# Two attentions of a four-layer network: the modulation product put one step later, a weight split one step sooner, and half a weight split behind the next row maxima

## The reference, cut to what matters

```python
for l in range(2):                                   # first network
    mod_lat = silu(c) @ w_ada[l] + b_ada[l]          # modulation: shift, scale, gate
    mod_ctx = silu(c_ctx) @ w_ada[l] + b_ada[l]
    xn = rms_norm(x, g_norm[l]) * (1 + sc) + sh      # the same for the context rows
    a, b, c_ = split_proj(xn @ w_in[l])              # three branches
    y_b = attend(q_rows, k_all, v_all) * silu(bz)    # softmax attention, 8 heads of 64
    x = x + gt * (concat([y_a, y_b, y_c]) @ w_out[l])
x = rms_norm(x, g_final)
# second network, layer 0: causal attention, 16 heads of 64, with rotation of q and k
qkv = (rms_norm(h) @ w_qkv).reshape(B, S, 3, 16, 64)
q, k = apply_rope(qkv[:, :, 0]), apply_rope(qkv[:, :, 1])
o = softmax(mask(q @ k.T / 8)) @ v
h = h + o @ w_o                                      # then a gated feed-forward layer
# layer 1: latent attention and a second feed-forward layer
```

## Time and profile before

| | |
|---|---|
| median of 3 runs | 1080.47 us (1080.44 to 1082.03) |
| profiled execution, whole | 1080.5 us |
| its span | 1078.6 us |
| PE / DVE / ACT / POOL busy | 99% / 67% / 53% / 13% |
| first attention, steps 0 to 18 | about 194 to 270 us |
| second attention | about 487 to 576 us |

### The profile page before, as it was taken

The page is one execution under the profiler, slowest core; times in us unless marked ns, Lnnn a source line. Parts: engine busy times, 40 slices in busy tenths (PEclk is TensorE's granted clock), DMA queues, the critical chain, the costliest instruction groups (busy, mean ns, idle before and its releaser), DMA issues.

```text
span 1078.6 us, 19909 instructions
## 1 busy us (share of the span) xinstructions
PE 1067.6 (99%) x8094; PEld 950.8 (88%) x8094; DVE 717.5 (67%) x1223; ACT 572.1 (53%) x970; POOL 141.2 (13%) x166
## 2 busy tenths in 40 slices
PE   9999999999999999999999999999999999999998
PEld 7887878656898998799899999999997799999997
DVE  4664566386554868768865676666677776766674
ACT  4532666544444566766565554444574555444454
POOL 0000010253210000632531000000023410000000
PEclk9999999999999999999999999999999999999999
DMA  9732221287513442057454364555543334555551
GB/s 384 315 126 74 77 78 40 94 286 250 189 43 118 143 141 79 2 196 234 147 167 153 121 235 160 193 184 172 195 154 112 124 118 157 196 195 174 214 180 39
DMA packets 25386, 168.77 MB, mean 156 GB/s; under 512 B 3280, under 2 KB 3536, under 8 KB 5456
## 3 DMA queue, kind: packets, MB, share of 16 engines
q1 hardware_dynamic: 25152, 167.25, 43.9%
q10 hardware_dynamic: 144, 0.26, 0.1%
HBM read 164.35 MB, written 1.05 MB: 153 GB/s over the span
## 4 chain that ended last, share of the span: by engine, by line
PE 91%; DVE 3%; ACT 2%; POOL 1%; DMA 1%; issue 1%; SPq 0%; DVEq 0%; ACTq 0%
PE bank L421 25%; PE bank L422 25%; PE bank L423 24%; PE bank L1633 2%; PE bank L478 2%; PE bank L1498 2%; PE bank L1653 2%; PE bank L1643 1%; DVE wlo L415 1%; DMA raw<-in_stream 1%; PE bank L1525 1%; PE bank L2296 1%; POOL TILE L1594 1%; ACT TILE L1687 1%; PE bank L1516 1%
## 5 line engine op out<-in xcount | busy, mean ns | idle before, releaser
L421 PE MATMUL bank<-OPH,whi 128*128 128x256 f32 (+1 forms) x1716 | 519.8, 303 | 0.6 <-DVE wlo L415 0.3
L423 PE MATMUL bank<-OPH,wlo 128*128 128x256 f32 (+1 forms) x1716 | 511.2, 298 | 0.0
L422 PE MATMUL bank<-OPL,whi 128*128 128x256 f32 (+1 forms) x1716 | 511.2, 298 | 0.0
L415 DVE TENSOR_TENSOR wlo<-raw,whi 128x1024 fp32r<-128x1024 f32 (+1 forms) x256 | 305.5, 1236 | 103.5 <-ACT whi L400 103.4
L421 PEld LDWEIGHTS bank<-OPH,whi 128*128 128x128 f32 x1716 | 328.0, 191 | 18.3 <-issue 5.6
L422 PEld LDWEIGHTS bank<-OPL,whi 128*128 128x128 f32 x1716 | 328.1, 191 | 9.9 <-issue 1.2
L423 PEld LDWEIGHTS bank<-OPH,wlo 128*128 128x128 f32 x1716 | 328.0, 191 | 9.8
L400 ACT ACTIVATE whi<-raw 128x1024 fp32r<-128x1024 f32 (+1 forms) x256 | 255.9, 1050 | 73.2 <-PE bank L423 72.4
L421 PE MATMUL bank<-whi,OPH 128*128 128x256 f32 (+2 forms) x272 | 93.7, 344 | 0.6 <-DVE OPL L695 0.6
L422 PE MATMUL bank<-wlo,OPH 128*128 128x256 f32 (+2 forms) x272 | 91.1, 335 | 0.0
L423 PE MATMUL bank<-whi,OPL 128*128 128x256 f32 (+2 forms) x272 | 91.0, 335 | 0.0
(11 more groups left out here) (279 smaller groups left out, 1122.4 us busy)
## 6 DMA issues: line engine op xcount, KB each, us to landing
raw<-in_stream SPq DMA_DIRECT2D x143, 1024.0 KB, 4.9
PROJ<-in_stream SPq DMA_DIRECT2D x5, 1024.0 KB, 18.0
raw<-in_stream SPq DMA_DIRECT2D x4, 1056.0 KB, 7.7
PROJ<-PROJ SPq DMA_DIRECT2D x32, 64.0 KB, 3.8
FIRST<-in_first SPq DMA_DIRECT2D x1, 1248.0 KB, 6.1
C<-in_con SPq DMA_DIRECT2D x1, 1157.5 KB, 7.3
FIRST<-in_first SPq DMA_DIRECT2D x1, 1024.0 KB, 8.1
WST<-in_w_s SPq DMA_DIRECT2D x2, 256.0 KB, 7.4
```

The source lines that it names most:

```text
L415: nc.vector.tensor_tensor(c.w[1][:, part], c.raw[:, part], c.w[0][:, part].bitcast(F32), ALU.subtract).then_inc(*raises(c.lo[h]))
L421: nc.tensor.matmul(out, w[0], x[0], start=start, stop=False, skip_group_check=skip)
L422: nc.tensor.matmul(out, w[0], x[1], start=False, stop=False, skip_group_check=skip)
L423: return nc.tensor.matmul(out, w[1], x[0], start=False, stop=stop, skip_group_check=skip)
```

## The change

The modulation step n now stands in attention step n+1 instead of n. The first `whi` half of `w_out` chunk 0 stands in modulation step 13 for ACT and its `wlo` half in step 14 for DVE, instead of both in step 15: in attention steps 14 and 15 instead of 15. In the second attention the DVE part of `q3` is parted: one half of `wlo` stays where it was, the other stands behind the maxima of pair 4.

```diff
             def step(self, e, who, n):
+                if who == "act" and n == self.steps - 4:
+                    split_hi(e, self.after.s + 0.5)
                 if who == "dve":
+                    if n == self.steps - 3:
+                        split_lo(e, self.after.s + 0.5)
                     if n % 2 == 0 and n > 0:
                         self.pairs[n // 2 - 1].add_bias(e)
                     if n % 2:
                         self.pairs[n // 2].copy_rows(e)
-                split = split_hi if who == "act" else split_lo
-                if n == self.steps - 2:
-                    split(e, self.after.s + 0.5)
...
-            def split_next(e, who, j):
+            def split_next(e, who, j, less=0):
                 if j.frees_head:
                     split_ahead(e, who, j.head[1].s + 1 + SPLIT)
                 for c, *_ in j.parts:
                     if c is not None and c.used == j.u.full:
-                        split_ahead(e, who, c.s + 1 + SPLIT)
+                        split_ahead(e, who, c.s + 1 + SPLIT - less)
...
+                if what == "half" and who == "dve":
+                    self.product.split_next(e, who, self.product.jobs[i], 0.5)
...
-                if l == 0 and j < mod.steps:
-                    attend_step(f"attn{l}_chunk", "chunk", mod, j)
+                if l == 0 and 0 < j <= mod.steps:
+                    attend_step(f"attn{l}_chunk", "chunk", mod, j - 1)
...
+        half_low = [(qkv_jobs, ("half", qkv.at["q3"]))]
-                F("q3"), w_(1), A("q3"), s_(3), Ra(2), Ra(6), Rb(2), Rb(6), t_(2), n_(3), M(XN[3]), V_("q3"),
-                F("k3"), A("k3"), s_(4), t_(3), V_("k3"), n_(4),
+                F("q3"), w_(1), A("q3"), s_(3), Ra(2), Ra(6), Rb(2), Rb(6), t_(2), n_(3), M(XN[3]), half_low,
+                F("k3"), A("k3"), s_(4), V_("q3"), t_(3), V_("k3"), n_(4),
```

## The result

| | before | changed |
|---|---|---|
| median | 1080.47 us (5 runs, 1080.44 to 1082.03) | 1085.45 us (5 runs, 1084.09 to 1086.93) |
| profiled execution, its span | 1080.5, 1078.6 us | 1085.69, 1083.9 us |
| mean granted clock of TensorE, single runs | 0.999 to 1.000 | 0.995, 0.997, 0.997, 0.998, 0.995 |

The changed kernel is slower by 4.98 us, ratio 1.0043, 95% interval 1.0033 to 1.0054. The sign was forecast; the size was twice the forecast (+2.45), and the time lies outside the range.

A forecast was written before the change was run, and what follows sets the result against it. PE, busy 99% of the span, was taken to bound the kernel, so only its waits counted. First attention +2.1 and second +0.35 made +2.45 us on 1080.5: 1082.9 us, range 1080.5 to 1084.3.

The forecast's parts named there:

- What bounds the kernel: Whole kernel: PE is busy 99% of the span, so only its waits or less work for it move the end.
- The three waits of the earlier trace: First attention, steps 5, 9 and 13: PE's waits for exponentials go, 3 x 0.31 = -0.93 us.
- steps 4, 8 and 12: First attention: these lose the turning of rows; step 4 shrinks to 3.58 us, just over the 3.54 the bank needs.
- The 0.34 ahead of the opening: First attention: PE's wait for `wlo` ahead of the first output product goes, -0.34 us.
- the wait for the bank: First attention, output product's opening: PE newly waits for DVE to copy the last modulation rows from bank 0, +0.8 us.
- The chain of the late load: First attention: `w_out` load lands at 260.74, delaying ACT's half and copy; PE waits at block 14, head 1, +2.55 us.
- Second attention: PE's gain of 0.98 us at pair 3 turns into a net loss of 0.35 by pair 5; bounds -0.98 to +0.95.
- The wait at the turning of pair 3: Second attention: PE's wait for POOL goes because DVE is idle beside POOL's last scaling, -0.98 us.
- The copies: Second attention: group 7's swap copies land at 548.5, POOL and DVE meet, pair 5 gets its data 0.35 us later than before.
- The first (copies in time): Second attention: swap copies are timely or POOL and DVE do not hinder each other, keeping -0.98; 1081.6 us, chance 0.24.
- The second: First attention: ACT's half finds its data, costing -0.5 there; about 1079.4 us in all, chance 0.06.
- The third (a slow queue): Both attentions: weight load lands 5.3 and last swap copy 5.7 us after issue; 1083.9 us, chance 0.15.

The follow-up runs named there:

- the filled run: Changed kernel plus 7 unread products ahead of the turning of block 14, head 1, in the unwritten half of the row bank: 1082.89 us, 1.0020.
- experiment 5: Kernel before with modulation one step later, both weight halves split in modulation step 15, output product opened whole in step 17: 1079.29 us, 0.9984.
- experiment 6: Kernel before with only the output product opened whole in step 17: 1080.79 us, 1.0000; also experiment 5 with it opened in two parts: 1081.72 us.
- the second edit's own run: Kernel before with only the second attention's edit, the first attention unchanged: 1080.63 us, ratio 0.9997.

## Why the prediction was right or wrong

**What bounds the kernel** was right as far as it went: all of the difference sits in waits of PE and in what they led to. It failed in the silent assumption behind the sum: that a wait of PE costs its own length, and PE's work afterwards what it cost before. Of the views that I read, the granted clock had been 1.00 throughout, and no rival asked what a wait longer than any of the earlier trace rows would do to it. That term was +2.5 to +2.7 in the changed kernel's profile; the filled run (clock at 1.00, the same chain of waits) shows it.

**What is won.** The three waits of the earlier trace rows are gone, as said. One of 0.52 that I had not seen came at the scores of block 7, behind step 6: the prediction asked only of steps 4, 8 and 12 what the loss of the turning does, but every even step lost it. It spoils little: the scores of block 14 begin at 253.79, 1.86 sooner than the 255.01 of before once the late start of 0.64 is added, and 1.00 of that is the multiplication not yet made. So the term is -0.86 (-0.93).

The 0.34 ahead of the opening is gone too, and the wait for the bank stands in its place, as the sum had it. That the term is real shows in the clean version of experiment 5, which gives 1.33: more than the 0.86 alone. Where only the opening was moved, the wait came back at the gate (experiment 6).

**What is paid.** The chain of the late load is right in each link. The load is issued at 256.58, which is 255.94 less the late start of 0.64 (forecast 255.84), ACT's half starts 4.86 after it (4.9), after an idle time of 4.51 ("some 4"), PE waits 2.45 (2.55) for the copy and 0.86 (0.8) for the bank. By these idle times the sum is -0.86 - 0.34 + 2.45 + 0.86 = +2.11, the +2.1 of the forecast. The filled run, whose clock stayed up, has +2.46. Of the 0.35 between them, 0.18 is that its turning was held longer (head 1 began 3.07 behind head 0, in the changed kernel 2.89); the rest is mostly that a wait costs some 0.1 to 0.2 more than its recorded idle time, as 0.24 cost 0.31 in the prediction. That the shift can be had without the two waits is shown by experiment 5.

**Second attention.** The wait at the turning of pair 3 went and PE was 0.98 ahead, as forecast: pair 4's scores are at 550.19 in the changed kernel, 4.60 behind before, where the shift had been 5.58. The copies did come late and POOL and DVE met (1.57 and 1.80). The size was off: the copies were there at 553.2, which less 5.58 is 547.6 and not 548.5, so the last took 4.2 and not 5.1, just under the lowest value of the earlier trace rows; the reciprocal came 0.14 late (558.73 - 5.58 against 553.01) and not 0.79, and PE waited 0.38 and not 1.3. The net is -0.26 instead of +0.35; in the second edit's own run it is +0.17, so one profile settles this small term only to some 0.4.

**The rivals.** The first (copies in time) was half right in its number and wrong in its reason: the copies were late. The second is refuted by the wait of 4.51. The third (a slow queue) came nearest to the time, but no load or copy was slow. The term that made the time was in none of them, which is why the range was too narrow on its upper side. The rule on the anatomy of one DMA in the Trainium skill (DMA: Bandwidth & Descriptors) holds where the copies stand alone in the queue, 2.2 us measured for an estimate of 2.2; the page gives it for transfers that GpSimd issues, these are SP's, and it says nothing of a copy behind a load of 1 MB, which took twice that.

**Open.** Why the clock stays low for 6.8 us in one run and 3.4 in another, and falls behind 2.06 us of idle time only sometimes, no trace here shows. Nor does one show whether the two slower filled runs had the fall, and behind which wait. How much of the start's 0.64 us is chance was not tried; other runs have 0.0 to 1.0 of it with and without the edits.

## What to carry to other kernels

When a change makes the busiest engine wait for longer than it does anywhere in the trace, its clock after the wait is a term of the sum, with its own price: here 0.8 to 2.7 us behind a wait of 2.1 to 2.7, up to as much as the wait itself, and not in every run. Before a weight split is moved up, work out when its data land, since all that stands behind it on the in-order engine is held too. And a short transfer that many wait for belongs ahead of a large load in the queue, not behind it.

## What the runs showed of the hardware

TensorE's granted clock went from 2.4 to 1.2 GHz 1.0 us after its return from a wait of 2.45 us, 2.4 after one of 2.51, 0.6 after one of 2.66, and within one of 2.84; it stayed low for 3.4 us in two of these profiles and 6.8 in the other two, and kept its level in the profile with 1.07 and 0.88 us of idle time 1.4 us apart and in the one with 2.06. In the stretch, the same 16 products took 1.98 instead of 1.09 us; 6.8 us of it cost 2.7, 3.4 us cost 1.5. Small copies of 64 KB landed 2.2 us after their issue alone and 4.5 to 4.8 behind a load of 1 MB that was issued 0.4 us before them.
